# PEER subkeys laid out by the host with the query dimension first, loaded straight to where the score products read them

## The chip, the core and the metric

The kernel runs on one NeuronCore of a Trainium2 chip. TensorE (PE) multiplies matrices into PSUM, VectorE (DVE) and ScalarE (ACT) work element by element, GpSimd (POOL) and SyncE (SP) mainly issue DMAs here. A core has 16 DMA engines, shared by all that it issues. The metric is the device time of one launch in microseconds; lower is better.

## The reference

One inference step of a two-layer decoder with d = 1024, for 512 prompt rows and 8 sample rows, all in float32. Layer 0 mixes with a short gated convolution and dilated attention, layer 1 with causal pooling. After each mixer comes a retrieval of experts:

```python
q = (hb @ wq).reshape(chunk, PEER_HEADS, 2, PEER_HALF)
s = jnp.einsum('nhcd,hckd->nhck', q, sk)          # sk: subkeys (8, 2, 128 keys, 128)
sv, si = lax.top_k(s, PEER_TOPK)                   # 16 per half, then 16 of the 256 sums
...
expert = i1 * N_KEYS + i2
g = jax.nn.softmax(cs, axis=-1)
act = gelu(einsum('nd,nhkd->nhk', hb, u_tab[expert]))
out = einsum('nhk,nhkd->nd', g * act, v_tab[expert])
```

Every row thus reads 8 x 16 rows of u and v per layer. The score product sums over the query dimension d, which the subkeys as given have last.

## The kernel before

**Stages.** An opening does the mixer of layer 0 for the first two 128-row tiles and the samples and the first query and score products. Then comes the gather stage: 66 tasks (33 a layer: 4 tiles by 8 heads, and one for the samples) of 16 steps, 8 for the samples. A step is called a use, and is numbered task x 16 + k in the agenda. In each, POOL's indirect DMA fetches one u|v row (8 KB) for each of 128 partitions into one of 8 ring slots (L922); DVE forms the dot product with the row of H (`product`, L2019); ACT makes act_h, gate and a diagonal matrix (L1481, L1486, L1490); PE multiplies the diagonal by the v half into an accumulator in PSUM (four instruction rows, L1291). When PE is done, the slot is free and POOL issues the next gather. Two of 16 uses of the first two tiles of layer 0 are added by DVE instead.

**What sets the order.** All else is cut into pieces, such as ("q", l, b, hc) for a chunk of the query projection of layer l and pair of tiles b, ("sc", ...) for its score product, ("squares", e, j), ("root", e), ("normed", e, j) for the parts of norm e. `whole_pieces` lists them with weights. The opening's pieces run in the order of the list. The rest go by `agenda`, which spreads each pair's list over a stretch of uses in proportion to the weights: those of layer 1, tiles 0 and 1, up to the first query chunk lie from use 320 to use 400. PE runs a piece in the use that the agenda names, ACT one later, DVE three later (`DVE_LAG`). Each engine runs its own instructions in order and waits on semaphores. After the diagonal of k = 2 ACT also makes the next task's softmax (`gates`, L1468 and L1469, with a table load ahead and one behind). DVE adds a finished accumulator to X at k = 3 (`add_unit`, L2050).

**Banks.** `psum_jobs` gives each piece that writes PSUM the next of five banks, of four from ("hT", 3, 0, 0) on.

**The subkeys.** The host gives a key-first array (2, 128 keys, 16, 128 d). SP loads layer 0's 1 MB to `sk_nat0`, in SC, at the piece ("scored_sample",), and layer 1's to `sk_nat1`, in HT, at ("squares", 4, 0) (L826). PE turns them in four pieces ("skT", l, j) of four 128x128 transposes (`transposes`, L956), and ACT copies each from PSUM to SKT (`copy_out`, L1344). The score products read SKT (L1279, and L1270 for the first two). The opening's skT pieces stand ahead of ("so", 7), the last of eight sample products with the cached values (`sample_output`, L1072), which wait for their cache rows (`load_kv`, L758 to L760). After it come the rest of the attention and the output projection ("wo", L974).

Of the kernel before, what the change touches and what calls it, by code (L numbers as in the profile page):

```python
# [30 lines left out]
P = 128  # L31
# [4 lines left out]
B = 8  # L36
L = 2
# [6 lines left out]
HC = 2 * PH  # L44
# [55 lines left out]
def whole_pieces(l, b):  # L100
# [23 lines left out]
    if (l, b) == (0, 0):  # L124
        transposed(e)
        for kind in "qk":
            for c in range(CA):
                out.append((("p", b, kind, c), 2.8))
            if kind == "q":
                out.append((("small",), 1))  # L130
        for c in range(CA):
            out.append((("p", b, "v", c), 2.8))
        for j in range(BT):
            out.append((("kn", b, j), 1))
        out.append((("own",), 1))
        for j in range(BT):
            out.append((("vn", b, j), 1))
        out.append((("vs",), 1))
        for kind in ("attend", -1), ("exp", 0), ("count", 0):
            out.append(((kind[0], b, kind[1]), 1))  # L140
        gated = [("p", b, kind, c) for kind in "cxb" for c in range(CA)]
        for m in range(BT * NH + 1):
            out.append((("attend", b, m), 0.9))
            out.append((("exp", b, m + 1), 0.9))
            if m == 8:
                out.append((("scored_sample",), 1))
                out.append((("tails", b), 1))
            if m < 12:
                out.append((gated[m], 2.8))
            if m == NH:  # L150
                out.append((("yT", b, 0), 0.3))
            out.append((("count", b, m + 1), 0.9))
            if m < 8:
                out.append((("qrep", m), 1))
            elif m == 8:
                out.append((("weighed",), 0))
            else:
                if m == 9:
                    out.append((("weights",), 1))
                for n in OUTPUTS_AT.get(m, ()):  # L160
                    if n == B - 1:
                        out.extend((("skT", 0, j), 1) for j in range(4))
                    out.append((("so", n), 1))
                if m == BT * NH - 1:
                    out.append((("masked",), 1))
                if m == BT * NH:
                    out.append((("gathered",), 1))
        for c in range(KD):
            out.append((("wo", b, c), 2.8))
            if c in (4, KD - 1):  # L170
                for j in (*range(BT), "s"):
                    out.append((("wt", b, j, c // 7), 1))
    elif l == 0:
        transposed(e)
        for kind in "qk":
            for c in range(CA):
                out.append((("p", b, kind, c), 2.8))
        for c in range(CA):
            out.append((("v", b, c), 2.8))
        for j in range(BT):  # L180
            out.append((("kn", b, j), 1))
        for kind in ("attend", -1), ("exp", 0), ("count", 0):
            out.append(((kind[0], b, kind[1]), 1))
        gated = [("p", b, kind, c) for kind in "cxb" for c in range(CA)]
        for m in range(BT * NH + 1):
            out.append((("attend", b, m), 0.9))
            out.append((("exp", b, m + 1), 0.9))
            if m < 12:
                out.append((gated[m], 2.8))
            if m == NH:  # L190
                out.append((("yT", b, 0), 0.3))
            out.append((("count", b, m + 1), 0.9))
        out.append((("tails", b), 1))
        for c in range(KD):
            out.append((("wo", b, c), 2.8))
    else:
        for j in range(BT):
            for half in range(2):
                out.append((("pp", b, j, half), 2))
        if b == 1:  # L200
            out.append((("pps",), 3))
        for j in range(BT):
            for half in range(2):
                out.append((("pl", b, j, half), 3))
        if b == 1:
            out.extend([(("pl", b, BT, 0), 2), (("pl", b, BT, 1), 2)])
        out.append((("mixed", b), 2))
    if (l, b) == (1, 0):
        for j in range(4):
            out.append((("skT", l, j), 1))  # L210
    norm(e + 1)
    transposed(e + 1)
    out.append((("q", l, b, 0), 3))
# [134 lines left out]
def jobs_of(piece):  # L348

    kind = piece[0]  # L350
    if kind in ("hT", "qa", "sa", "yT", "p", "v", "kn", "vn", "vs", "wo", "wt", "skT", "pp", "pps", "pl", "q", "sc"):
        return [piece]
    if kind == "small":
        return [("conv_state",), ("conv_w",)]
    if kind == "own":
        return [("kns",), ("qns",)]
    if kind == "tails":
        return [("us",)] if piece[1] == 0 else [("utail",)]
    if kind == "attend":
        b, m = piece[1:]  # L360
        out = []
        if m + 1 < BT * NH:
            out.append(("s", b, m + 1))
        if 0 <= m < BT * NH:
            out.append(("pT", b, m))
        if m == BT * NH:
            out.append(("yT", b, BT - 1))
        return out
    if kind == "qrep":
        return [piece]  # L370
    if kind in ("rep", "gain"):
        return [(kind, piece[1], half) for half in range(2)]
    if kind == "scored_sample":
        return [("ssT",)]
    if kind == "weights":
        return [("spT",)]
    return []
# [42 lines left out]
def build(nc, x_prompt, x_sample, state_conv, state_win_k, state_win_v, state_pool, norm_mix, w_in_ab,  # L420
# [5 lines left out]
    with ctx:  # L426
# [77 lines left out]
        o += KV  # L504
        masked = RING[0:B * NH, o:o + DA]
        o += DA
        sk_nat0 = SC[:, 0:HC * P].rearrange("p (h d) -> p h d", h=HC)
        block_step = B * NH + NH
        SPT_all = RING[:, o:o + 2 * B * block_step]
        SPT_blocks = SPT_all.rearrange("p (t b n) -> p t b n", t=2, b=B)[:, :, :, 0:NH]  # L510
# [50 lines left out]
        pscale = VN[:, 0:2, :].rearrange("p a n -> p (a n)")  # L561
        pbias = VN[:, 2:4, :].rearrange("p a n -> p (a n)")
        HTf = HT[:, :, :].rearrange("p k n -> p (k n)")
        sk_nat1 = HTf[:, 0:HC * P].rearrange("p (h d) -> p h d", h=HC)
        pstate = HTf[:, 0:D]
        SCt = SC[:, 0:T * HC * NK].rearrange("p (t h k) -> p t h k", t=T, h=HC)
        sc64 = SC[:, T * HC * NK:T * HC * NK + 2 * NK]
# [145 lines left out]
        def _(sp):  # L713
# [48 lines left out]
            def front(piece):  # L762
# [30 lines left out]
                    store(conv_sample[0, :, 0, :], state_conv[0, :, 1, :])  # L793
                    store(pool_sample[0, :, 0:PS - 1, :], state_pool[0, :, 1:PS, :])
                if piece == ("scored_sample",):
                    sp.dma_start(sk_nat0, peer_subkeys[0]).then_inc(sk_loaded, 16)
                if kind == "qrep":
                    load_kv(piece[1] + NKV)
                if kind == "so" and piece[1] + NKV < B:
# [21 lines left out]
                if piece == ("squares", 4, 0):  # L821

                    wait_emptied(sp, ("yT", 1, BT - 1))
                    wait_full(sp, ("q", 0, 1, HC - 1))
                    sp.wait_ge(stored, stores[0])
                    sp.dma_start(sk_nat1, peer_subkeys[1]).then_inc(sk_loaded, 16)  # L826
                    sp.dma_start(poolw, pool_w[0]).then_inc(pool_loaded, 16)
                    sp.dma_start(pscale, pool_scale[0:1, :].to_broadcast([P, D])).then_inc(pool_loaded, 16)
                    sp.dma_start(pbias, pool_b.rearrange("o g n -> o (g n)").to_broadcast([P, D])).then_inc(pool_loaded, 16)
                if piece == ("squares", 6, 0):  # L830
                    wait_full(sp, ("q", 1, 0, HC - 1))
                    sp.dma_start(pstate[0:B * PS, :], state_pool[0].rearrange("b j n -> (b j) n")).then_inc(state_loaded, 16)
# [104 lines left out]
        def _(pe):  # L937
# [202 lines left out]
            def front(piece):  # L1140
# [85 lines left out]
                if kind == "wt":  # L1226
# [2 lines left out]
                        wait_emptied(pe, ("wo", b, c))  # L1229
                    at, n = (BN, B) if j == "s" else (j * P, P)  # L1230
                    transposes(piece, P, [HT[:, c, at:at + n] for c in range(4 * half, 4 * half + 4)])
                if kind == "skT":
                    l, j = piece[1:]
                    pe.wait_ge(sk_loaded, 16 * (l + 1))
                    nat = (sk_nat0, sk_nat1)[l]
                    transposes(piece, P, [nat[:, 4 * j + c, :] for c in range(4)])
                if kind == "pp":
                    b, j, half = piece[1:]
                    pe.wait_ge(rows_normed, rows_by(4 + 2 * b, j + 1))
# [10 lines left out]
                if kind == "q":  # L1250
                    l, b, hc = piece[1:]
                    if hc == 0 and opens:
                        wait_rows(l, b, 4 * l + 2 * b + 1)
                        for j in range(4):
                            wait_emptied(pe, ("skT", l, j))
                    across(piece, opens, HT_N if has_sample(l, b) else BN, lo=tile_done(l, b, hc) * P)
                if kind == "qa":
                    for half in range(2):
# [4 lines left out]
                        last = nc.tensor.matmul(out[:, 0:P], w[k], HT[:, k, 0:P], start=(k == 0), stop=(k == KD - 1))  # L1263
                    close_bank(last, piece)
                if kind == "sa":
                    for j in range(4):
                        wait_emptied(pe, ("skT", 0, j))
                    wait_emptied(pe, ("qa", piece[1]))
                    out = open_bank(piece)
                    close_bank(nc.tensor.matmul(out[:, 0:P], qp[:, piece[1], 0:P], SKT[:, piece[1], :],  # L1270
# [62 lines left out]
        def _(act):  # L1333
# [38 lines left out]
            def front(piece):  # L1372
# [21 lines left out]
                if kind == "hT":  # L1394
# [2 lines left out]
                        copy_out(piece, HT[:, :, BN:HT_N], wide(piece, KD, B))  # L1397
                    else:
                        copy_out(piece, HT[:, 4 * half:4 * half + 4, j * P:(j + 1) * P], wide(piece))
                if kind == "skT":  # L1400
                    copy_out(piece, SKT[:, 4 * piece[2]:4 * piece[2] + 4, :], wide(piece))
                if kind == "p" and piece[2] in "cqk":
                    b, k, c = piece[1:]
                    big, small, scale = {"c": (uT[:, c, 2:UW], c_s, 1.0), "q": (qT[:, c, :], qT_s, HD ** -0.5),
# [111 lines left out]
        def _(dve):  # L1516
# [581 lines left out]
            for piece in opening()[0][1:]:  # L2098
# [2 lines left out]
                    for part in range(3):  # L2101
                        search(part, SC[:, 0:NT], 0, 0, False)
                if piece == ("sa", 1):
                    for j in range(4):
                        wait_emptied(dve, ("skT", 0, j))
                    dve.wait_ge(own_stored, 48)
                    dve.sem_inc(ring_cleared, 1)
                    first_search()
# [66 lines left out]
```

## Time and profile before

| | |
|---|---|
| three runs | 2989.9, 2994.02, 3000.66 us; median 2994.02 |
| profiled execution, span | 2990.9 us, 26454 instructions; its own time is given by no other figure |
| PE, DVE, ACT, POOL busy | 87%, 69%, 43%, 41% of the span |
| DMA | 1214.85 MB, mean 406 GB/s |
| first gather | issued at 220.7 us |

The profile is one execution: the engines' busy time, the DMA traffic, and the chain of work that ended last, followed back from the end. A line number is that of kernel.py before the change.

### The profile page before, as it was taken

To read this page: it belongs to the slowest core of one execution; us is meant where nothing else is said; L and a number is where in the kernel's file an instruction comes from. 1 tells how busy PE (TensorE), PEld (TensorE's weight loads), DVE (VectorE), ACT (ScalarE), POOL (GpSimd) and SP (SyncE) were. 2 spreads that over 40 slices of the span, in tenths; PEclk is the share of its full clock that TensorE was granted. 3 is DMA by queue.
4 is the path that set the end of the run, shared out by engine and by line. 5 is a ranking of instruction groups with operands and counts; after the bars stand their busy time and mean duration, and the time that the engine had idled before them with its cause. 6 is when DMAs were issued, how large, how long until landed. Compare 5 with 4: busy or idle time off the path is not lost.

```text
span 2990.9 us, 26454 instructions
## 1 busy us (share of the span) xinstructions
PE 2588.8 (87%) x7305; PEld 1275.3 (43%) x7305; DVE 2077.1 (69%) x4938; ACT 1284.4 (43%) x3756; POOL 1227.3 (41%) x1104
## 2 busy tenths in 40 slices
PE   8989998999888888888988889888999978777786
PEld 6675464555444443334444334333444422222222
DVE  2656767788766657776667677777676766677666
ACT  2123444655444434453444444445443444444444
POOL 2113443444444444444444444444344444444442
PEclk9999999999999999999999999999999999999999
DMA  9979999999999999999999999999999999999997
GB/s 353 329 289 389 391 421 408 419 400 416 421 421 421 421 421 416 421 400 421 422 421 420 407 403 407 421 421 421 421 420 420 418 420 409 419 421 411 421 420 325
DMA packets 174992, 1214.85 MB, mean 406 GB/s; under 512 B 19731, under 2 KB 20767, under 8 KB 33270
## 3 DMA queue, kind: packets, MB, share of 16 engines
q0 software_dynamic: 155904, 1124.11, 91.2%
q1 hardware_dynamic: 18941, 89.07, 7.7%
q8 instruction: 58, 0.95, 0.1%
q14 instruction: 89, 0.72, 0.1%
HBM read 1208.47 MB, written 38.37 MB: 417 GB/s over the span
## 4 chain that ended last, share of the span: by engine, by line
DMA 46%; PE 36%; DVE 7%; ACT 7%; issue 3%; POOL 1%; SPq 0%; ACTq 0%; DVEq 0%; POOLq 0%
DMA RING<-in_peer_uv,idx 44%; PE PSUM L1291 22%; PE PSUM L974 9%; DVE RING L2019 4%; ACT diag L1490 2%; ACT L1481 1%; ACT gate L1486 1%; DMA RING<-in_peer_uv,pidx 1%; POOL RING L922 1%; PE PSUM L985 1%; PE PSUM L956 1%; ACT act_h L1481 1%; ACT L1469 1%; PE PSUM L1279 1%; DVE X L2079 0%
## 5 line engine op out<-in xcount | busy, mean ns | idle before, releaser
L1291 PE MATMUL PSUM<-RING,diag 128*128 128x512 f32 (+1 forms) x4032 | 1951.2, 620 | 363.9 <-ACT diag L1490 356.9
L922 POOL DMA_INDIRECT RING<-in_peer_uv,idx x1024 | 1177.2, 1150 | 1563.3 <-PE PSUM L1291 1411.4
L2019 DVE CUSTOM_DVE_ANT_0 RING<-RING,H 128x1024 f32<-128x1024 f32 x1032 | 1262.5, 1224 | 701.6 <-DMA RING<-in_peer_uv,idx 683.2
L1291 PEld LDWEIGHTS PSUM<-RING,diag 128*128 128x128 f32 (+1 forms) x4032 | 726.9, 192 | 1424.9 <-ACT diag L1490 796.2
L1481 ACT ACTIVATE act_h<-dots 128x1 f32<-128x1 f32 x1040 | 208.2, 200 | 1119.1 <-DVE dots L2019 1117.2
L1490 ACT ACTIVATE diag<-ident,gate 128x128 f32<-128x128 f32 x992 | 398.3, 402 | 33.7 <-PE PSUM L1291 1.1
L974 PE MATMUL PSUM<-HT,WCH 128*128 128x256 f32 (+2 forms) x1408 | 334.8, 384 | 1.4 <-ACT HT L1344 1.3
L1486 ACT ACTIVATE gate<-act_h,ex 128x1 f32<-128x1 f32 x992 | 292.1, 295 | 32.2
L974 PEld LDWEIGHTS PSUM<-HT,WCH 128*128 128x128 f32 x1408 | 265.7, 192 | 93.9 <-issue 61.8
L1481 ACT ACT_TABLE_LOAD x91 | 116.8, 1283 | 5.4 <-DVE dots L2019 3.8
L1344 ACT ACTIVATE YT<-PSUM 128x256 f32<-128x256 f32 (+4 forms) x70 | 27.4, 391 | 168.2 <-PE PSUM L974 152.4
L2019 DVE DVE_READ_ACCUMULATOR2_ANT dots<- 128x1 f32 x1040 | 85.3, 82 | 0.0
L1469 ACT ACT_TABLE_LOAD x66 | 84.7, 1283 | 1.2
L1363 ACT ACTIVATE H<-H,negm 128x128 f32<-128x128 f32 (+3 forms) x32 | 18.0, 562 | 98.8 <-DVE negm L1722 97.7
L1279 PEld LDWEIGHTS PSUM<-SKT,YT 128*128 128x128 f32 (+1 forms) x316 | 42.6, 177 | 34.9 <-issue 30.8
L956 PE MATMUL PSUM<-ident,H 128*128 128x128 f32 (+1 forms) x200 | 36.3, 305 | 20.4 <-POOL POOL_STATE_M L871 9.7
L1279 PE MATMUL PSUM<-SKT,YT 128*128 128x128 f32 (+1 forms) x316 | 50.5, 284 | 0.0
L974 PE MATMUL PSUM<-HT,RING 128*128 128x264 f32 x192 | 46.8, 402 | 0.0
L956 PEld LDWEIGHTS PSUM<-ident,H 128*128 128x128 f32 (+1 forms) x200 | 25.2, 158 | 48.8 <-issue 18.4
L2000 DVE TENSOR_TENSOR onehot<-onehot,si 128x512 f32<-128x512 f32 x65 | 44.6, 687 | 0.0
L1997 DVE TENSOR_TENSOR onehot<-cij,iota 128x512 f32<-128x512 uint32 x65 | 44.6, 686 | 0.0
L2002 DVE TENSOR_REDUCE picked<-onehot 128x32 f32<-128x512 f32 x65 | 44.2, 680 | 0.0
(262 smaller groups left out, 1525.3 us busy)
## 6 DMA issues: line engine op xcount, KB each, us to landing
WCH<-in_peer_wq SPq DMA_DIRECT2D x28, 1024.0 KB
WCH<-in_w_in_ab SPq DMA_DIRECT2D x18, 1024.0 KB
RING<-in_peer_uv,idx POOLq DMA_INDIRECT x1024
out_win_k_sample<-in_state_win_k POOLq DMA_DIRECT2D x8, 2016.0 KB, 12.2
out_win_v_sample<-in_state_win_v POOLq DMA_DIRECT2D x8, 2016.0 KB, 10.8
RING<-in_w_in_ab SPq DMA_DIRECT2D x6, 1024.0 KB, 11.5
WCH<-in_w_out_ab SPq DMA_DIRECT2D x6, 1024.0 KB
X<-in_x_prompt SPq DMA_DIRECT2D x4, 512.0 KB, 9.1
```

What stands on the lines that cost most here:

```text
L922: pool.indirect_dma_start(rows[:, use % SLOTS, :], None, peer_uv.rearrange("l e n -> (l e) n"), bass.IndirectOffsetOnAxis(ap=at, axis=0),) ...
L956: last = nc.tensor.transpose(out[0:cols, n * width:n * width + rows], src, ident[0:rows, 0:rows])
L974: last = nc.tensor.matmul(out[:, lo:width], w[k], rows[:, k, lo:width], start=(k == 0), stop=(k == KD - 1))
L1279: last = nc.tensor.matmul(out[0:m, j * P:(j + 1) * P], qp[:, hc % 2, j * P:j * P + m], SKT[:, hc, :], start=True, stop=True)
L1291: last = nc.tensor.matmul(PSUM[0:out_n, accumulator(n) + half, :], diag[:, at % DIAGS, 0:out_n], rows[:, use % SLOTS, D + half * 512:D + h ...
L1469: nc.scalar.activation(ex[:, par, :], cs[:, par, :], ACT.Exp, bias=ncs[:, par:par + 1], accum_out=exsum[:, par:par + 1]).then_inc(gates_ex ...
L1481: chain(nc.scalar.activation(act_h[:, st, column], dots[:, st, column], ACT.Gelu))
L1486: chain(nc.scalar.activation(gate[:, st, column], act_h[:, st, column], ACT.Copy, scale=weight))
L1490: nc.scalar.activation(diag[:, at % DIAGS, 0:n], selector, ACT.Copy, scale=gate[:, st, column]).then_inc(diag_ready, 1)
L1997: left(V.tensor_tensor(onehot[:], cij[:].unsqueeze(3).to_broadcast([P, 2, TOP, TOP]), iota16[:].unsqueeze(1).unsqueeze(1).to_broadcast([P, ...
L2000: left(V.tensor_tensor(onehot[:], onehot[:], si[:].unsqueeze(2).to_broadcast([P, 2, TOP, TOP]), ALU.mult))
L2019: V.tensor_tensor_reduce(out=u, in0=u, in1=row, scale=1.0, scalar=0.0, op0=ALU.mult, op1=ALU.add, accum_out=dots[:, tau % SETS, k:k + 1]). ...
```

## The change

The host lays the subkeys out as (2, 128 d, 16, 128 keys). SP loads both layers' to SKT. The eight skT pieces go from all engines' lists, and what waited for their copies waits for the load. Layer 1's load moves behind the pool weights' three, and waits until the last score product of layer 0 has been written, since that still reads layer 0's subkeys in SKT. Each partition's part of the load is 8 KB in one run before and after, in HBM and in SBUF.

```diff
@@ whole_pieces
                 for n in OUTPUTS_AT.get(m, ()):
-                    if n == B - 1:
-                        out.extend((("skT", 0, j), 1) for j in range(4))
                     out.append((("so", n), 1))
...
-    if (l, b) == (1, 0):
-        for j in range(4):
-            out.append((("skT", l, j), 1))
     norm(e + 1)
@@ sync
                 if piece == ("scored_sample",):
-                    sp.dma_start(sk_nat0, peer_subkeys[0]).then_inc(sk_loaded, 16)
+                    sp.dma_start(SKT[:, :, :], peer_subkeys[0]).then_inc(sk_loaded, 16)
...
                     wait_emptied(sp, ("yT", 1, BT - 1))
-                    wait_full(sp, ("q", 0, 1, HC - 1))
                     sp.wait_ge(stored, stores[0])
-                    sp.dma_start(sk_nat1, peer_subkeys[1]).then_inc(sk_loaded, 16)
                     sp.dma_start(poolw, pool_w[0]).then_inc(pool_loaded, 16)
                     sp.dma_start(pscale, pool_scale[0:1, :].to_broadcast([P, D])).then_inc(pool_loaded, 16)
                     sp.dma_start(pbias, pool_b.rearrange("o g n -> o (g n)").to_broadcast([P, D])).then_inc(pool_loaded, 16)
+                    wait_full(sp, ("sc", 0, 1, HC - 1))
+                    sp.dma_start(SKT[:, :, :], peer_subkeys[1]).then_inc(sk_loaded, 16)
@@ tensor
-                if kind == "skT":
-                    l, j = piece[1:]
-                    pe.wait_ge(sk_loaded, 16 * (l + 1))
-                    nat = (sk_nat0, sk_nat1)[l]
-                    transposes(piece, P, [nat[:, 4 * j + c, :] for c in range(4)])
...
-                        for j in range(4):
-                            wait_emptied(pe, ("skT", l, j))
+                        pe.wait_ge(sk_loaded, 16 * (l + 1))
@@ scalar
-                if kind == "skT":
-                    copy_out(piece, SKT[:, 4 * piece[2]:4 * piece[2] + 4, :], wide(piece))
@@ host
-            a = _np.ascontiguousarray(a.transpose(0, 3, 1, 2, 4)).reshape(L, NK, HC, NK)
+            a = _np.ascontiguousarray(a.transpose(0, 4, 1, 2, 3)).reshape(L, NK, HC, NK)
```

**The opening, on PE.** The rows of the program before are, in order, the last attention transposes, the products with V, the subkeys' 16 transposes, and the last sample product (L1072), with what follows it.

```order
L956 MATMUL PSUM<-ident,H 128x128 x2
L1006 MATMUL PSUM<-VN,H 128x64 x2
L956 MATMUL PSUM<-ident,SC 128x128 x16
L1072 MATMUL PSUM<-RING 64x512 x2
L956 MATMUL PSUM<-ident,H 128x128 x2
L1006 MATMUL PSUM<-VN,H 128x64 x4
L956 MATMUL PSUM<-ident,SC 128x128 x4
L1033 MATMUL PSUM<-ident,RING 128x8
```

The same place after the change, with line numbers lower by 7:

```order
L949 MATMUL PSUM<-ident,H 128x128 x2
L999 MATMUL PSUM<-VN,H 128x64 x2
L1065 MATMUL PSUM<-RING 64x512 x2
L949 MATMUL PSUM<-ident,H 128x128 x2
L999 MATMUL PSUM<-VN,H 128x64 x4
L949 MATMUL PSUM<-ident,SC 128x128 x4
L1026 MATMUL PSUM<-ident,RING 128x8
```

The row of 16 is gone and nothing else has moved. The agenda of layer 1 has: with four fewer pieces between uses 320 and 400 the others spread wider. The pieces ahead of the gap come up to six uses later than before ("mixed", from 368 to 374), the gain and norm 5 behind it one or two uses earlier ("squares", 5, 0 and 1 from 384 and 385 to 382 and 383; ("root", 5) from 386 to 384).

**Norm 5, on ACT.** First before the change; diag is the diagonal of a use, rstd<-ss the root, ex the softmax of the next task.

```order
L1490 ACTIVATE diag<-ident,gate 128x128
L1468 ACTIVATE ncs<-cs 128x1
L1469 ACT_TABLE_LOAD
L1469 ACTIVATE ex,exsum<-cs,ncs 128x16
L1481 ACT_TABLE_LOAD
L1481 ACTIVATE act_h<-dots 128x1
L1486 ACTIVATE gate<-act_h,ex 128x1
L1490 ACTIVATE diag<-ident,gate 128x128
L1393 ACT_TABLE_LOAD
L1393 ACTIVATE rstd<-ss 128x5
L1481 ACT_TABLE_LOAD
L1481 ACTIVATE act_h<-dots 128x1
```

After the change, with line numbers lower by 14 or 16:

```order
L1474 ACTIVATE diag<-ident,gate 128x128
L1379 ACT_TABLE_LOAD
L1379 ACTIVATE rstd<-ss 128x5
L1465 ACT_TABLE_LOAD
L1465 ACTIVATE act_h<-dots 128x1
L1470 ACTIVATE gate<-act_h,ex 128x1
L1474 ACTIVATE diag<-ident,gate 128x128
L1452 ACTIVATE ncs<-cs 128x1
L1453 ACT_TABLE_LOAD
L1453 ACTIVATE ex,exsum<-cs,ncs 128x16
L1465 ACT_TABLE_LOAD
L1465 ACTIVATE act_h<-dots 128x1
```

The root has changed places with the softmax: it now stands one use ahead of it instead of one behind.

**Norm 5, on DVE.** RING,dots is a use's dot product, ss<-X a row sum of squares, X<-PSUM the addition of a finished accumulator. Before:

```order
L2019 ISA RING,dots<-RING,H 128x1024
L2019 ISA dots 128x1
L2050 TENSOR_TENSOR X<-PSUM,X 128x512 x2
L2000 TENSOR_TENSOR onehot<-onehot,si 128x512
L1547 ISA H,ss<-X 128x1024
L1547 ISA ss 128x1
L2019 ISA RING,dots<-RING,H 128x1024
L2019 ISA dots 128x1
L2002 TENSOR_REDUCE picked<-onehot 128x32
L1547 ISA H,ss<-X 128x1024
L1547 ISA ss 128x1
L1552 TENSOR_SCALAR ss<-ss 128x5
```

After, with line numbers lower by 16:

```order
L1531 ISA H,ss<-X 128x1024
L1531 ISA ss 128x1
L2003 ISA RING,dots<-RING,H 128x1024
L2003 ISA dots 128x1
L1981 TENSOR_TENSOR onehot<-cij,iota 128x512
L1531 ISA H,ss<-X 128x1024
L1531 ISA ss 128x1
L1536 TENSOR_SCALAR ss<-ss 128x5
L2003 ISA RING,dots<-RING,H 128x1024
L2003 ISA dots 128x1
L2034 TENSOR_TENSOR X<-PSUM,X 128x512 x2
```

Both sums of squares now stand ahead of the addition instead of behind it, in the two uses before.

## Rows read from the trace of the kernel before

**Rows 1.** The page: span and instructions, DMA traffic, chain that ended last.
```profile
span 2990.9 us, 26454 instructions
...
DMA packets 174992, 1214.85 MB, mean 406 GB/s; under 512 B 19731, under 2 KB 20767, under 8 KB 33270
...
DMA 46%; PE 36%; DVE 7%; ACT 7%; issue 3%; POOL 1%; SPq 0%; ACTq 0%; DVEq 0%; POOLq 0%
```

**Rows 2.** The gather stage: us, busy time of each engine (instructions), granted clock, DMA share, GB/s.
```profile
core 0: us, PE busy (x) PEld busy (x) DVE busy (x) ACT busy (x) POOL busy (x), PEclk, DMA share, GB/s
...
221.00:2965.00 2744.00, 2376.76 (x6369) 1123.64 (x6367) 1957.45 (x4620) 1230.92 (x3615) 1193.78 (x1040) 0.97 1.01 415
```

**Rows 3.** Timeline before the output projection: start, length, engine, line, operation, idle before.
```profile
146.78 0.47 SPq L760 DMA_DIRECT2D RING<-in_state_win_v  x1
...
155.29 1.92 PE L956 MATMUL PSUM<-ident,SC 128*128 128x128 f32 x16
...
156.32 2.04 ACT L1344 ACTIVATE SKT<-PSUM 128x512 f32<-128x512 f32 x4
...
157.88 1.93 PE L1072 MATMUL PSUM<-RING 128*64 128x512 f32 x4 [0.67 <-DMA RING<-in_state_win_v]
```

**Rows 4.** One microsecond at the start of the output projection, columns as in rows 2.
```profile
166.00:167.00 1.00, 1.00 (x3) 0.79 (x4) 0.97 (x2) 0.00 (x0) 0.62 (x1) 0.50 1.05 332
```

**Rows 5.** TensorE's timeline there: the projection's first 64 instructions, and its last 48.
```profile
165.97 15.88 PE L974 MATMUL PSUM<-YT,WCH 128*128 128x264 f32 x64 [0.59 <-DVE YT L1810]
...
186.55 10.85 PE L974 MATMUL PSUM<-YT,RING 128*128 128x264 f32 x48
```

**Rows 6.** TensorE's timeline: one subkey turn of layer 1, a stall, the first query product.
```profile
1277.91 0.60 PE L956 MATMUL PSUM<-ident,HT 128*128 128x128 f32 x4
...
1303.52 3.78 PE L1291 MATMUL PSUM<-RING,diag 128*128 128x512 f32 x4 [3.19 <-ACT diag L1490]
...
1323.74 1.89 PE L974 MATMUL PSUM<-HT,WCH 128*128 128x256 f32 x8
```

**Rows 7.** Stretches of 25 us of the gather stage, columns as in rows 2.
```profile
1140.00:1165.00 25.00, 22.29 (x62) 10.01 (x61) 22.18 (x54) 12.40 (x36) 15.28 (x12) 0.97 1.00 404
1265.00:1290.00 25.00, 23.18 (x58) 9.20 (x57) 18.10 (x50) 11.89 (x36) 13.73 (x11) 1.00 1.01 421
1290.00:1315.00 25.00, 18.87 (x41) 7.52 (x40) 22.00 (x47) 14.53 (x37) 8.37 (x9) 0.80 0.92 370
1315.00:1340.00 25.00, 23.03 (x68) 11.70 (x67) 17.03 (x41) 13.45 (x40) 15.81 (x12) 1.00 1.01 409
```

**Rows 8.** VectorE's and then ScalarE's timeline around the norm behind the second mixer.
```profile
1293.68 1.23 DVE L2019 CUSTOM_DVE_ANT_0 RING<-RING,H 128x1024 f32<-128x1024 f32 x1 [0.65 <-DMA RING<-in_peer_uv,idx]
...
1294.84 1.28 DVE L2050 TENSOR_TENSOR X<-PSUM,X 128x512 f32<-128x512 f32 x2
...
1296.63 1.22 DVE L1547 CUSTOM_DVE_ANT_0 H<-X 128x1024 f32<-128x1024 f32 x1
...
1292.46 0.20 ACT L1481 ACTIVATE act_h<-dots 128x1 f32<-128x1 f32 x1 [1.52 <-DVE dots L2019]
...
1293.33 0.19 ACT L1468 ACTIVATE ncs<-cs 128x1 f32<-128x1 f32 x1
...
1296.54 0.20 ACT L1481 ACTIVATE act_h<-dots 128x1 f32<-128x1 f32 x1
...
1300.98 0.21 ACT L1393 ACTIVATE rstd<-ss 128x5 f32<-128x5 f32 x1 [2.18 <-DVE ss L1552]
...
1302.50 0.20 ACT L1481 ACTIVATE act_h<-dots 128x1 f32<-128x1 f32 x1
```

**Rows 9.** SyncE's queue after the first pair of tiles' last query product.
```profile
1095.97 0.37 SPq L826 DMA_DIRECT2D HT<-in_peer_subkeys  x1
...
1151.08 0.25 SPq L744 DMA_DIRECT2D G<-in_norm_ffn  x1
```

**Rows 10.** TensorE's timeline: the last score products of that pair of tiles.
```profile
1101.07 1.05 PE L1279 MATMUL PSUM<-SKT,YT 128*128 128x128 f32 x8
```

More of the change, by code:

```diff
@@ L350, in jobs_of @@
     kind = piece[0]
-    if kind in ("hT", "qa", "sa", "yT", "p", "v", "kn", "vn", "vs", "wo", "wt", "skT", "pp", "pps", "pl", "q", "sc"):
+    if kind in ("hT", "qa", "sa", "yT", "p", "v", "kn", "vn", "vs", "wo", "wt", "pp", "pps", "pl", "q", "sc"):
         return [piece]
@@ L506, in build @@
         o += DA
-        sk_nat0 = SC[:, 0:HC * P].rearrange("p (h d) -> p h d", h=HC)
         block_step = B * NH + NH
@@ L563, in build @@
         HTf = HT[:, :, :].rearrange("p k n -> p (k n)")
-        sk_nat1 = HTf[:, 0:HC * P].rearrange("p (h d) -> p h d", h=HC)
         pstate = HTf[:, 0:D]
@@ L1265, in front @@
                 if kind == "sa":
-                    for j in range(4):
-                        wait_emptied(pe, ("skT", 0, j))
+                    pe.wait_ge(sk_loaded, 16)
                     wait_emptied(pe, ("qa", piece[1]))
@@ L2103, in _ @@
                 if piece == ("sa", 1):
-                    for j in range(4):
-                        wait_emptied(dve, ("skT", 0, j))
                     dve.wait_ge(own_stored, 48)
```

## Prediction

> **What bounds the kernel now.** Read the page first, for the span and what the chain that ended last consists of: 46% of it is DMA and 36% PE [rows 1]. Then cut the span into stretches. The gather stage, from 221 to 2965 us, takes 2744 us of the 2990.9, and in it the DMA engines' share is 1.01 at 415 GB/s [rows 2]. One gather is 128 x 8 KB, 1.05 MB, so at the 421 GB/s of an undisturbed stretch [rows 7] a use takes 2.49 us. Nothing that PE, DVE or ACT save there shortens the stage, unless it fills one of the lapses in which the rate falls. The opening, up to the first gather, is another matter: there work on PE stands in series, and a microsecond off it starts the whole stage a microsecond earlier. So three places are read in detail: the timeline of PE around the layer 0 turn of the subkeys [rows 3], that around the layer 1 turn [rows 6], and the lapse at norm 5, which the agenda shifts [rows 7, 8].
>
> **The opening.** Removed are 16 transposes on PE, 1.92 us from 155.29, and four copies on ACT, 2.04 us from 156.32. What PE does next is the last sample product, L1072 at 157.88, and it had sat idle 0.67 us before it, released by the DMA of a cached-value tile whose last part SP issued at 146.78 [rows 3]. Without the transposes PE comes to that wait at about 155.3 and waits 157.88 - 155.29 = 2.6 us instead of 0.67. The product starts when it did. The copies lie beside that wait and product. The cover is the DMA: if the tile landed before 155.3, the gain would be the whole 1.9 us. But the load in question is queued behind the same transfers before and after, and the subkeys' own 1 MB is issued at the same piece, in the same 8 KB runs, so I take the landing as unchanged: 0, with -1.9 as the bound below.
>
> The bound above is the clock. At the start of the output projection the granted clock is 0.50 of full, 1.2 instead of 2.4 GHz [rows 4], after waits such as that of 0.67 us. The projection's first 64 instructions took 15.88 us; at the pace of the last 48, 10.85 us, they would take 14.47 [rows 5]. One such fall thus costs 1.4 us. With the transposes gone PE idles 1.9 us more just ahead of this, so a fall could come there as well: +1.4. It could as well only come earlier, in place of the one now paid, which is why I take 0. The Trainium skill (TensorE: Matmul & The Clock Gate, What's actually happening) speaks against this edit: the half clock is the default and activity lifts it, so removed filler work can be paid back in clock. By that page alone the sum would be 0 or +1.4; the trace agrees in so far as the fall shown follows waits.
>
> **Layer 1's turn.** Four pieces of four transposes, 0.60 us of PE each [rows 6], so 2.4 us of PE, and four copies on ACT of 0.5 us each (2.04 / 4, [rows 3]). They lie in a stretch with a DMA share of 1.01 at 421 GB/s [rows 7]: the gathers hide them. Worth 0. If the cover were gone, it would be 2.4 us.
>
> **The load and its new wait.** Layer 1's load was issued at 1095.97; the score products that it must now wait for end at 1101.07 + 1.05 = 1102.1 [rows 9, 10]. Behind it on SP is the gain load of norm 5, at 1151.08 [rows 9], 49 us later, and the query product that needs SKT starts at 1323.74 [rows 6], 222 us later. The three pool loads now stand ahead of it and go out some 0.4 us earlier, by the 0.37 us that its own issue took. The same megabyte moves. 0.
>
> **The shifted agenda.** This is the one edit with a sign of its own. At norm 5 the stream lapses: 370 GB/s in 1290 to 1315 and 409 in the next 25 us [rows 7]; (421 - 370) x 25 / 421 = 3.0 us and 0.7 us, 3.7 us in all. The cause is a queue on two engines. The dot product of use 387 starts at 1293.68; then DVE adds an accumulator (1.28 us), makes a search step, and starts the first sum of squares at 1296.63 [rows 8]. ACT meanwhile has made the softmax and, with a table load before and behind it, is back at 1296.54; then it waits for both sums and makes the root at 1300.98, and act_h of use 388 comes at 1302.50. Without a disturbance a product starts every 2.49 us, and act_h follows 1.27 us after it (1292.46 for the product one step ahead of 1293.68). Use 388's should have come at 1293.68 + 2.49 + 1.27 = 1297.44, so it was 5.1 us late.
>
> After the change the sums stand in uses 385 and 386, ahead of the addition. From the start of product 385: product 1.2, a small search step 0.3 to 0.4 by the 0.5 of the one between 1296.12 and 1296.63, squares 1.2, so 2.8; then product 1.2, search step 0.6, squares 1.2, scaling 0.2, so 6.0 us to the root. Root and table load take 1.5 (1300.98 to 1302.50), so act_h of 386 comes at 7.5 instead of 3.8: 3.7 late. But now the softmax follows at once: 0.87 us of that use's own work (1292.46 to 1293.33) and 3.2 of softmax with its tables (1293.33 to 1296.54) put act_h of 387 at 11.6, where 2 x 2.49 + 1.27 = 6.25 was due: 5.35 late. The peak thus changes from 5.1 to 5.4, and the lapse by +0.3 us. Bounds: the lapse vanishes, -3.7; or the whole softmax group stands in it unhidden, +3.2. Norm 4 shifts by one use; its stretch, 1140 to 1165, ran at 404 GB/s, a loss of 1.0 us [rows 7], so -1.0 to +1.0, and I take 0. The pooling products of layer 1, moved by up to six uses, lie in full stream: 0. The banks that every later piece gets change by one, the reuse distance doesn't: 0.
>
> **The sum.** 0 + 0 + 0 + 0.3 = +0.3 us against the profiled 2990.9, which is 3.1 below the median of the three runs, 2994.02. I carry the change over to the median: 2994.3 us.
>
> **The rivals.** *Nothing to measure* is the forecast: between -3 and +4 us. For it speaks that each removed instruction has a named cover. Its own range is 2990 to 2999.
>
> *Faster after all.* The tile wait is not what holds PE (-1.9), the half clock at 166 goes too (-1.4), both lapses close (-3.7, -1.0): -8.0, 2986. For it: 4.3 us of PE work do leave, and PE is 36% of the chain. Against: 0.67 us of idle right behind the first turn, and the full stream around the second. Even this is under the 9 us that count; it needs luck in the runs to show.
>
> *Slower through norm 5.* The root with its two table loads and the softmax with its own now follow each other one use apart on ACT, with one diagonal between; PE starves for both, its clock falls as it did in 1290 to 1315 (0.80), and the ring of 8 slots drains. Price: +3.2, 2997.2 us. It decides the sign as soon as ACT's lateness at 387 goes beyond the 5.1 us of now; to be measurable the lapse would have to grow from 3.7 to 12.7 us. Against that: DVE's addition, 1.28 us, has left the way of the root.
>
> *SP is held up.* The new wait blocks SP's queue. It costs nothing until the last score product is more than 49 us late, and SKT's reader is only held from 222 us on; at 60 us of hold, the norm and its 11 us would follow, 3005. Nothing in the rows comes near it.
>
> *The change doesn't do what it says.* Were the new layout slower to load, the opening would have to wait for it; but SKT's first reader comes after the projection, and 1.05 MB in 8 KB runs is what was moved before.
>
> **How the numbers follow.** About 0.3%, 9 us, is what a measurement of this kernel can tell from no change; the three runs alone differ by 10.8. Forecast 0.90; faster rival 0.04; norm 5 0.04; SP 0.01; layout 0.01. The first rival ends just short of 9 us and the third well short, so faster by over 0.3% gets 0.04 and slower 0.05, with the scatter of the runs in both; within it 0.91. For the range: the bounds of the terms add to -1.9 - 3.7 - 1.0 = -6.6 and +1.4 + 3.2 + 1.0 = +5.6, that is 2987.4 to 2999.6; the runs' own scatter takes it to 2986.5 and 3001.
>
> **What the profile would show.** Right: the last sample product still released by the DMA, with an idle time of about 2.6 us, and the first gather within 1.5 us of where it is, at the start of the stretch in [rows 2]; layer 1's subkeys issued at about 1102; the stream at 421 GB/s through 1265 to 1285; a lapse of 3 to 5 us around use 386, root and softmax side by side on ACT. Wrong: the first gather 1.9 us or more earlier, a half clock ahead of the sample product, the lapse gone or doubled, or an idle PE before the first query product of layer 1. The forecast fails if a transfer in the opening lands otherwise than before, since that wait alone decides whether 1.9 us count.

## The result, and the profile after

The changed kernel takes 2996.88 us (median of 22 runs, 2992.06 to 3001.56), the one before 2993.46 us (22 runs, 2988.14 to 3000.66). The ratio is 1.0012, 95% interval [1.0006, 1.0017]: 3.4 us slower, inside the 0.3% that was called no measurable change, and clear of zero all the same. A run's time is 1.9 to 2.0 us above its span (2998.55 for the span of 2996.6 below).

The page of the kernel after, to be read beside [rows 1]; as there, the lines are span, DMA traffic and the chain that ended last:

```profile
span 2996.6 us, 26362 instructions
...
DMA packets 174991, 1214.85 MB, mean 405 GB/s; under 512 B 19730, under 2 KB 20766, under 8 KB 33269
...
DMA 48%; PE 35%; DVE 7%; ACT 6%; issue 3%; POOL 1%; SPq 0%; ACTq 0%; POOLq 0%; DVEq 0%
```

There are 92 instructions fewer and the same megabytes. The timeline of the changed kernel on TensorE, at the place of [rows 3] (start, length, line, operation, idle before and its releaser):

```profile
159.04 1.93 PE L1065 MATMUL PSUM<-RING 128*64 128x512 f32 x4 [3.07 <-DMA RING<-in_state_win_v]
...
163.95 0.38 PE L1026 MATMUL PSUM<-ident,RING 8*128 8x8 f32 x2
```

As forecast, the last sample product is still released by the cached-value tile; PE now rests 3.07 us ahead of it, and the product still takes 1.93 us. At the norm that the agenda moved, VectorE's sums and then ScalarE's instructions (the page's lines lower by 14 or 16), to be read beside [rows 8]:

```profile
1294.05 1.23 DVE L2003 CUSTOM_DVE_ANT_0 RING<-RING,H 128x1024 f32<-128x1024 f32 x1 [0.84 <-DMA RING<-in_peer_uv,idx]
...
1299.85 0.21 ACT L1379 ACTIVATE rstd<-ss 128x5 f32<-128x5 f32 x1 [2.27 <-DVE ss L1536]
...
1301.37 0.20 ACT L1465 ACTIVATE act_h<-dots 128x1 f32<-128x1 f32 x1
...
1302.44 1.28 ACT L1453 ACT_TABLE_LOAD   x1
...
1304.15 1.28 ACT L1465 ACT_TABLE_LOAD   x1
1305.45 0.20 ACT L1465 ACTIVATE act_h<-dots 128x1 f32<-128x1 f32 x1
```

The product of use 385 starts at 1294.05, and use 386 gets its act_h at 1301.37, 7.3 us later (forecast 7.5). Then the softmax follows, with a table load on either side, and use 387 gets its act_h at 1305.45, 11.4 us after 1294.05 (forecast 11.6). Yet the stream's stretches there, beside [rows 7], in the same columns, show a smaller lapse:

```profile
1140.00:1165.00 25.00, 21.25 (x51) 8.90 (x50) 21.22 (x49) 14.76 (x41) 12.82 (x11) 0.93 1.01 419
1265.00:1290.00 25.00, 21.07 (x45) 7.57 (x45) 17.01 (x42) 9.61 (x31) 10.79 (x11) 1.00 1.01 422
1290.00:1315.00 25.00, 19.09 (x43) 7.22 (x43) 21.82 (x43) 14.82 (x39) 10.46 (x9) 0.86 0.98 389
1315.00:1340.00 25.00, 23.74 (x70) 12.01 (x70) 17.73 (x50) 11.13 (x37) 12.46 (x11) 1.00 1.00 419
```

(421 - 389 + 421 - 419) x 25 / 421 = 2.0 us, where it was 3.7. The stretch of norm 4, 1140 to 1165, ran at 419 GB/s where it had 404. SyncE's queue after the change, beside [rows 9], and the last score products, beside [rows 10]:

```profile
1107.43 0.33 SPq L822 DMA_DIRECT2D SKT<-in_peer_subkeys  x1
1159.64 0.25 SPq L737 DMA_DIRECT2D G<-in_norm_ffn  x1
```

```profile
1106.35 1.05 PE L1265 MATMUL PSUM<-SKT,YT 128*128 128x128 f32 x8
```

The load goes out when the score products end, 52 us ahead of SP's next. Nothing in these rows is slower. The two profiles' spans differ by 5.7 us. The first gather has 1.45 of them (222.17 against 220.72), and 1.16 of those were there when the last sample product started (159.04 against 157.88). The rest, 4.3 us, lies in the gather stage. One profile of each can't tell more: PE's clock falls at other moments in every execution, and in the changed one a fall happened to lie at 690 us, with a lapse behind it (690 to 740: clock 0.90 and 384 GB/s, 1.00 and 414 before). So the cause was looked for in kernels that hold one part of the change each, timed over 11 or 12 runs, and in the same stretch of all their profiles.

### The profile page after: what moved, and what is told of

The parts are those of the page before. It is cut to its first block, busy times and chain, and to the rows that moved or that the text cites. A ratio compares the mean times of both kernels' runs of the same rounds, so it can differ in the third digit from the quotient of the medians.

```text
span 2996.6 us, 26362 instructions
## 1 busy us (share of the span) xinstructions
PE 2595.6 (87%) x7273; PEld 1274.9 (43%) x7273; DVE 2077.4 (69%) x4938; ACT 1281.8 (43%) x3748; POOL 1228.6 (41%) x1104
## 4 chain that ended last, share of the span: by engine, by line
DMA 48%; PE 35%; DVE 7%; ACT 6%; issue 3%; POOL 1%; SPq 0%; ACTq 0%; POOLq 0%; DVEq 0%
DMA RING<-in_peer_uv,idx 46%; PE PSUM L1277 21%; PE PSUM L967 9%; DVE RING L2003 4%; ACT diag L1474 2%; ACT L1465 1%; ACT gate L1470 1%; DMA RING<-in_peer_uv,pidx 1%; PE PSUM L949 1%; ACT act_h L1465 1%; PE PSUM L1265 1%; ACT L1453 1%; POOL RING L915 1%; PE PSUM L978 1%; PE PSUM L988 0%
## 5 line engine op out<-in xcount | busy, mean ns | idle before, releaser
L1839 DVE COPY SC<-PSUM 128x256 f32<-128x256 f32 (+1 forms) x64 | 26.1, 408 | 26.8 <-PE PSUM L1265 26.8
```

## The experiments

**One part each.** First the kernel before with layer 0's part alone, then with layer 1's alone. Only the host's layout of one layer, its load and its waits are changed, for instance

```diff
-                        out.extend((("skT", 0, j), 1) for j in range(4))
...
-                    sp.dma_start(sk_nat0, peer_subkeys[0]).then_inc(sk_loaded, 16)
+                    sp.dma_start(SKT[:, :, :], peer_subkeys[0]).then_inc(sk_loaded, 16)
```

> Kernel before with only layer 0's subkeys loaded straight; layer 1 keeps its load, its turn on PE and the agenda. The changed kernel was 1.0012 of before, 3.4 us. Opening theory: the 1.9 us of PE work that left the opening turned into waiting and moved or added a half-clock stretch, so this kernel holds most of the 3.4 us: 1.0005 to 1.0010 of before. Bank theory: the shift by one PSUM bank of every later piece (it is in this kernel too) costs, around the switch from five to four banks at norm 3: 1.0010. Agenda theory: all of it comes from norm 5's new place: 1.0000 here.

Measured: 1.0004 [0.9996, 1.0013].

> Kernel before with only layer 1's subkeys loaded straight: the opening is untouched and so are the banks; the agenda of layer 1, its turn on PE and its load are as after the change. Agenda theory: root and softmax follow each other on ACT, the lapse of the gather stream near use 386 grows, 1.0005 to 1.0012 of before. Opening theory and bank theory: 1.0000 or a little under.

Measured: 1.0004 [0.9994, 1.0014]. The times alone don't tell the two parts apart: each interval holds 1.0000, and the two excesses add to 0.0008 where the whole change has 0.0012.

**Agenda and banks.** The changed kernel with four empty pieces that hold the agenda's old places:

```diff
         out.append((("mixed", b), 2))
+    if (l, b) == (1, 0):
+        for j in range(4):
+            out.append((("gap", l, j), 1))
```

> Changed kernel with four empty pieces in the place of layer 1's turns in the list, so that every other piece has the use that it had before. Agenda theory: the loss goes, 1.0000 of before. Opening theory and bank theory: it stays, 1.0010. If the measured 1.0012 is a sum of small terms, 1.0006.

Measured: 1.0005 [0.9996, 1.0013]. And with the old banks:

```diff
                 for n in OUTPUTS_AT.get(m, ()):
+                    if n == B - 1:
+                        out.extend((("gap", 0, j), 1) for j in range(4))
...
         at = (at + 1) % (NB if i < cut else NB - 1)
+        if name[0] == "gap":
+            continue
```

> Changed kernel in which the rotation of PSUM banks skips four places where the turns of layer 0 were, so that every piece has the bank that it had before; agenda and loads as changed. Bank theory: the loss goes, 1.0000 of before. Opening and agenda theories: it stays at 1.0012.

Measured: 1.0008 [1.0000, 1.0017], 2995.67 us. The bank theory expected 1.0000, the very edge of this interval, so this run alone speaks against it without excluding it. So do the kernels with fillings below: the one with 16 transposes has the new banks and is at 0.9995, and the one with four fillings is no slower than the kernel before with three, which has the old banks. The agenda theory is neither shown nor excluded by 1.0005.

It is the profiles that decide the agenda theory, which wants a longer lapse. The sum that gave 3.7 us before and 2.0 after, over 1290 to 1340, gives 2.7 to 3.7 us in the four kernels here that have the old places (the kernel before, layer 0 alone, the old agenda, and the kernel before with fillings) and 1.4 to 3.0 us in the ten with the new ones. The lapse got shorter, by 1.0 us on average, so it isn't where 3.4 us went.

What these profiles do show is the clock. Here is the same stretch of three kernels, 155 to 212 us, from the last sample product to the first score products (columns as in [rows 2]: the third figure from the end is the granted clock). Before the change:

```profile
155.00:212.00 57.00, 50.24 (x256) 42.19 (x255) 25.28 (x66) 13.01 (x32) 4.89 (x8) 0.91 0.83 315
```

Layer 0's part alone, and 13 us of it by themselves:

```profile
155.00:212.00 57.00, 49.18 (x214) 40.52 (x215) 23.95 (x61) 10.38 (x26) 4.92 (x8) 0.83 0.81 311
```

```profile
158.00:171.00 13.00, 11.57 (x38) 8.89 (x37) 4.30 (x13) 0.98 (x2) 1.69 (x3) 0.50 1.00 362
```

Layer 1's part alone has 0.91, as before.

The changed kernel with the old banks:

```profile
155.00:212.00 57.00, 47.02 (x202) 37.28 (x202) 24.54 (x64) 10.38 (x25) 4.89 (x8) 0.84 0.84 317
```

and TensorE's timeline in it:

```profile
159.91 3.67 PE L1071 MATMUL PSUM<-RING 128*64 128x512 f32 x4 [4.03 <-DMA RING<-in_state_win_v]
...
167.74 0.59 PE L1032 MATMUL PSUM<-ident,RING 8*128 8x8 f32 x2
```

After 4.03 us of rest the product takes 3.67 us instead of the 1.93 of [rows 3], and the small products behind it 0.59 us a pair instead of the 0.38 of the changed kernel's own profile above: PE is at 1.2 GHz instead of 2.4 (the granted clock is 0.50 from 160 to 176 us). In the kernel before and in layer 1's part alone, where the turns are in place, the product takes 1.93 us.

**Filling the rest.** If PE's rest is the cause, work that nobody needs must repair it. The changed kernel, with transposes of the identity into a bank that is free then:

```diff
+FILL = 16
...
                 if kind == "so":
+                    if piece[1] == B - 1:
+                        for n in range(FILL):
+                            nc.tensor.transpose(PSUM[:, 6, n % 4 * P:(n % 4 + 1) * P], ident[:], ident[:])
                     sample_output(piece[1])
```

> Changed kernel with 16 transposes of the identity (1.9 us of PE) in the opening where layer 0's turns were; they go to a PSUM bank that nothing reads then, and nobody waits for them. Clock theory: what the missing turns cost is PE's rest, which brings a half-clock stretch into the sample product and what follows; with the filler back the product runs at 1.93 us again, the first gather comes 1 to 3 us earlier than in the changed kernel, the ratio to before falls from 1.0012 to about 1.0004. Rival, the place of norm 5 and its collision on ACT: no change, 1.0012. Rival, the load's landing: no change either, and PE's idle time ahead of the sample product 0.7 us instead of 2.3 to 4.

Measured: 0.9995 [0.9987, 1.0004], 2991.86 us; its interval lies below that of the changed kernel. Its timeline and stretch:

```profile
157.02 1.93 PE L1066 MATMUL PSUM<-RING 128*64 128x512 f32 x4 [1.53 <-DMA RING<-in_state_win_v]
```

```profile
155.00:212.00 57.00, 49.33 (x246) 40.91 (x245) 24.76 (x67) 10.81 (x27) 4.89 (x8) 0.91 0.81 308
```

16 instructions of no use make the kernel faster: the two ratios differ by 0.0017, about 5 us, and their intervals allow 2 to 8 us (an estimate from the two intervals, which come from different sets of runs). Within its own set its median is 3 to 4 us below those of the three kernels that follow, which have no filling. The rivals expected no change. The profile has the product at 1.93 us and goes 63.1 us from it to the first gather, as the changed kernel's own profile does; against the 65.8 us that kernels without turns take on average (table below) that is 2.8 us.

**Two attempts at the wait itself.** The last sample product later (`OUTPUTS_AT`, 14 to 15 for its entry), and the loads of x later:

```diff
-                if kind == "so" and piece[1] in (4, 5):
-                    t = BT + piece[1] - 4
+                if piece == ("masked",):
+                    sp.wait_ge(so_done, B)
                     wait_full(sp, ("vs",))
...
```

> Changed kernel with the last sample product moved behind the last attention transpose and the products with V of the step before: useful work of about 1 us stands where PE waited for the cached values. Clock theory: shorter rest and about 1 us less behind the product, 1.0000 to 1.0004 of before, first gather 1 to 3 us earlier than in the changed kernel. Norm 5 theory: only the 1 us of reordering, 1.0009.

Measured: 1.0006 [0.9997, 1.0014]. The rest was only split: 1.48 us ahead of the attention transposes and 0.39 ahead of the product, which took 3.02 us. The first gather went out at 222.48, not 1 to 3 us earlier than the changed kernel's 222.17: that expectation missed, and in time nothing can be told from the changed kernel.

> Changed kernel in which SP issues the loads of the second pair of tiles of x (1 MB) only when the last sample product is done, so that they don't share the DMA engines with the last cached-value tile. If that sharing is what makes the tile land 11 us after its issue, it lands 1 to 2.5 us earlier, PE's idle time ahead of the product falls from 2.3 to 4 us to under 1.5, and the kernel is at 1.0000 to 1.0004 of before. If the copies of the caches that POOL issues are what it shares with, nothing changes.

Measured: 1.0008 [1.0000, 1.0017]. This expectation failed. The tile's last part was issued at 146.52 and the product started at 158.14, 11.6 us later, as against 157.88 - 146.78 = 11.1 before [rows 3]: the loads of x are not what it waits for. (In the fourteen profiles of this case that part lands 10.0 to 12.7 us after its issue.) POOL's copies of the caches, 2016 KB each, run beside it in all these kernels; whether they are it wasn't tried.

> Changed kernel with both of these. Clock theory: PE hardly rests, the turns' 1.9 us are won after all: 0.9990 to 0.9997 of before, first gather at 217 to 219 us. Norm 5 theory: 1.0000 to 1.0005, since the collision stays.

Measured: 1.0013 [1.0003, 1.0023]. A miss of both expectations: the two edits together repair nothing. PE rested 1.48 us ahead of the attention transposes and 0.63 ahead of the product, which took 2.92 us, and the mean clock of the stretch was 0.82, the lowest of all. So splitting the rest doesn't keep the clock up.

**Filling all the rests.** The opening has other waits behind this one, the longest that for norm 1's first row. The edit adds a `busy` with the loop above and calls it ahead of the last turned attention rows (6), of norm 1's rows (24), of the last sample product (16) and of the output projection (4):

```diff
+            def busy(bank6, n):
+                for i in range(n):
+                    nc.tensor.transpose(PSUM[:, bank6, i % 4 * P:(i % 4 + 1) * P], ident[:], ident[:])
...
+                        busy(6, 6)
...
+                            busy(7, 24)
...
+                        busy(6, 16)
...
+                            busy(7, 4)
```

> Changed kernel with transposes of the identity, which nobody waits for or reads, in four of PE's waits of the opening: 16 ahead of the last sample product, 6 and 4 in the two waits behind it, 24 (2.9 us) in the wait for norm 1's first row. Clock theory: the half-clock stretches from 158 to 212 us (3.4 and 6.8 us of them before the change, 10 to 20 in kernels without the turns) go or shrink to one; half of their length comes back while PE is busy, so 3 to 5 us below the kernel with the 16 alone (0.9995 of before): 0.998 to 0.9988, first gather at 215 to 218 us. Rival, where the 16 helped by chance of the runs: 0.9995 to 1.0012, first gather near 220 to 224.

Measured: 0.9987 [0.9979, 0.9996], 2988.27 us. Its timeline and stretch:

```profile
198.88 2.78 PE L954 MATMUL PSUM<-ident 128*128 128x128 f32 x24
```

```profile
155.00:212.00 57.00, 52.94 (x317) 44.92 (x316) 28.65 (x80) 12.16 (x30) 4.89 (x8) 1.00 0.84 318
```

The clock stays at 1.00 throughout this stretch, and the first gather goes out at 217.35 us.

> Changed kernel with the 24 transposes in the wait for norm 1's first row alone. Clock theory: the half clock from 203 to 212 us goes, up to 3.4 us back, but that around the sample product stays: 0.9998 to 1.0004. Rival: 1.0012.

Measured: 0.9994 [0.9985, 1.0002]. Somewhat better than expected; its stretch still has 0.88, since the clock fell around the sample product (3.81 us of rest, the product 3.60 us). In time this kernel can't be told from the one with the 16 (0.9995), although its rest ahead of the product is unfilled. So the times say that fillings help, and not that the place of the missing turns is the one that must be filled.

> The kernel with the four fillings, and 12 more transposes in each of the two waits for VectorE at 113 and 127 us (1.5 us each before the change). Clock theory: the half clock at 112 to 118 us goes too, 1 to 1.7 us: 0.9975 to 0.9985 of before. If these two waits are shorter than 12 transposes, the filling itself delays by up to 1 us and nothing is won over the four fillings.

Measured: 0.9977 [0.9968, 0.9986], 2985.93 us against 2991.99, faster than both kernels of the case and the lowest median here, though its interval overlaps that of the four fillings. The half clock at 112 to 118 us is gone, as expected: from 105 to 125 us the clock is 1.00, where it was 0.91 before and 0.83 with four fillings. The first gather goes out at 214.81 us. But with every one of these waits filled the clock fell all the same:

```profile
155.00:212.00 57.00, 53.96 (x311) 46.98 (x310) 29.25 (x85) 11.71 (x30) 4.43 (x8) 0.94 0.76 289
```

> Kernel before (with its turns) and the other three fillings, 6, 4 and 24. It stands to the first kernel of this set as before to after with the clock held up on both sides. Clock theory: the turns are hidden in the wait for the cached values, so both are alike within 0.0005, at 0.998 to 0.9988 of before. If the turns were on the path, this one is 1.9 us slower, 0.0006.

Measured: 0.9984 [0.9975, 0.9993], 2988.79 us. With the clock mostly held up on both sides (0.97 here, 1.00 without the turns) the kernels with and without the turns are alike, 2988.79 and 2988.27 us. They differ in their banks and in norm 5's place too, and no loss shows from these. The intervals reach 0.0008 to 0.0009 to either side, so these times don't exclude the 0.0006 of turns on the path. The profiles tell more: here PE waits another 1.04 us for the tile behind its turns, and before the change 0.67 us. Only in layer 1's part alone did the product follow its turns without a wait:

```profile
156.65 1.93 PE L1069 MATMUL PSUM<-RING 128*64 128x512 f32 x4
```

There the tile's last part, issued at 146.29, had landed 10.0 us later, some 0.3 us earlier than PE came to it. The turns are hidden but for that.

The openings side by side, each from one profile, in the order of the clock. The last column is the time from the start of the last sample product to the first gather, which leaves out what lies ahead of the edit:

| kernel | PE's rest ahead of the product, us | mean clock 155 to 212 | first gather, us | product to first gather, us |
|---|---|---|---|---|
| changed, four fillings | 1.02 | 1.00 | 217.35 | 58.5 |
| before (turns), three fillings | 1.04 | 0.97 | 215.53 | 60.0 |
| changed, six fillings | 0 | 0.94 | 214.81 | 61.6 |
| before (turns) | 0.67 | 0.91 | 220.72 | 62.8 |
| layer 1 only (turns) | 0 | 0.91 | 219.77 | 63.1 |
| changed, 16 transposes | 1.53 | 0.91 | 220.07 | 63.1 |
| changed | 3.07 | 0.91 | 222.17 | 63.1 |
| changed, product later | 1.48 and 0.39 | 0.88 | 222.48 | 63.6 |
| changed, norm 1's 24 alone | 3.81 | 0.88 | 221.77 | 64.6 |
| changed, x late | 2.93 | 0.86 | 223.96 | 65.8 |
| changed, old agenda | 2.29 | 0.85 | 220.60 | 65.7 |
| changed, old banks | 4.03 | 0.84 | 227.72 | 67.8 |
| layer 0 only | 2.61 | 0.83 | 223.37 | 66.5 |
| changed, both attempts | 1.48 and 0.63 | 0.82 | 222.00 | 65.9 |

The last column follows the clock from 58.5 us at 1.00 to 66 or 68 below 0.85, whichever edit brought the clock there. (In the two kernels with two rests the product stands about 1 us of work later, so theirs is that much short.) The five without turns or filling (changed, x late, old agenda, old banks, layer 0 only) average 65.8 us, the three with the turns or with the 16 transposes 63.0. From the first gather to the end of the span the fourteen profiles take 2767 to 2774 us, whatever their opening: before 2770.2, changed 2774.4, the longest. So an opening that ends later isn't made good behind it, and what the changed kernel's own profile lost, it lost mostly in the gather stage of that execution. Its opening is the mildest of the five, with 0.91 in spite of a rest of 3.07 us, which is why it showed nothing.

## Why the prediction was right, and where a term was off

**The opening's work.** Right: the DMA covers the 1.9 us. The tile's landing ends PE's wait in twelve of the fourteen profiles; in the other two (layer 1 only and six fillings) PE had turns or filling to do until it had landed, and 0.3 us of turns stuck out in the first. PE's rest was forecast at 2.6 us and was 3.07 in the changed kernel, 2.3 to 4.0 us in the five.

**The clock.** This is the mis-sized term. The working had it as a bound, +1.4 us for one more fall, and took 0, on the ground that a fall could come earlier instead of in addition. The runs showed more: the first gather came 223.56 - 220.19 = 3.4 us later on average (five profiles against three, which range over 220.6 to 227.7 and 219.8 to 220.7 us). 2.8 us of it lie behind the start of the product and go with the clock; the other 0.6 lie ahead of the edit. The loss in time is 3.4 us, and its interval is 1.8 to 5.1, so the size fits, but no run measures the clock's share of it by itself: layer 0's part alone, whose profile has a mean clock of 0.83, was only 1.0004 [0.9996, 1.0013] in time. Where the clock fell at the product, it lasted through the small products behind it and made them longer, and it was low at the start of the projection too (0.50 from 158 to 171 us in layer 0's part alone). So the fall came in addition, and the mean clock went from 0.91 to 0.83 to 0.86 in four of the five. The sentence from the Trainium skill (TensorE: Matmul & The Clock Gate, What's actually happening) that spoke against the edit was right, and its side of the sum, +1.4, was nearer than 0. The traces agree with it for the most part: in those four kernels the half clock came right behind the longer rest, and with the rests filled the mean was 1.00, 0.97 and 0.94. The changed kernel's own profile, 0.91 behind 3.07 us of rest, doesn't show it; its first gather moved by 1.45 us, just inside the 1.5 that were named as a sign.

**Layer 1's turn.** Right as far as it can be read: 421 and 422 GB/s in 1265 to 1290 with and without it.

**The load and its wait.** Right: issued at 1107.43, at the end of the score products, with 52 us to spare. (It was forecast for about 1102. The score products themselves came 5.3 us later in this profile, 1106.35 against 1101.07.)

**Norm 5.** The order on the engines was right to 0.2 us (7.3 and 11.4 against 7.5 and 11.6), the conclusion drawn from it was not: ACT's peak lateness stayed where it was (11.4 - 6.25 = 5.1 us, as before) and the lapse fell from 3.7 to 2.0 us, outside the 3 to 5 that were named as a sign. What was wrong is the step that turned a peak of lateness into lost DMA time one for one. The profiles of the other kernels bear it out with a gain of 1.0 us on average. The times can't resolve it: the kernel with the old agenda was if anything faster than the changed kernel (1.0005 against 1.0012, with overlapping intervals).

**Sum and chances.** 2994.3 was forecast from a median of three runs, 2994.02; from the 2993.46 of 22 runs the same +0.3 gives 2993.8, and the measured 2996.88 is 3.1 us above that. The clock term, 2.8 to 3.4 us by the openings against the 0 it was given, fills this as well as profiles of one execution each can say. The sign wasn't forecast. That the result lies within the 0.3% is owed to a threshold of 9 us, more than twice the term that was missing. The lower sum of the range left out the -1.4 that the rival "faster after all" counts; nothing hung on it. The rival "slower through norm 5" had 2997.2, close to the measured time by luck, since it named the wrong place. A slower clock ahead of the projection should have stood as a rival of its own, with 3 to 4 us.

## What to carry to other kernels

Before work is taken from TensorE, look at what it will do in that time instead: if it waits for a transfer, nothing is won, and the longer rest can cost the clock of the critical work behind it. A wait of a microsecond or more inside a series of matmuls is a place for transposes that nobody needs, and six such fillings brought the changed kernel from 3.4 us above the one before to 6 us below it. This gain doesn't belong to the change: three fillings brought the kernel before, with its turns, 3.2 us down. And where the clock falls at a different moment in every execution, a stretch must be compared over the profiles of several kernels; the changed kernel's own profile hid its cause.

## What was not expected of the hardware

16 transposes whose result is never read made a kernel faster, by 3 to 5 us. Splitting the same rest in two (1.48 and 0.39 us) didn't help: the product was still slowed, to 3.02 us from 1.93. The clock can fall or not behind the same kind of rest: 3.07 us left the product at 1.93 us in one profile, and 2.29 us slowed it to 2.78 in another. And 1 MB less of traffic beside a load left its landing time at 11.6 us in the one profile of it.
